# TensorE's expert loop rotated: down products first, slot addresses loaded two blocks ahead, covered waits dropped

## The reference, cut to what matters

```python
def moe(x2, w_router, router_bias, w1, w3, w2):
    expert_idx, gate_w = route(x2, w_router, router_bias)      # 2 of 16 experts for each of 512 tokens
    ...                                                        # tokens sorted by expert, padded to whole blocks
    def run_block(args):
        e, toks = args
        xb = x_pad[toks]
        h = jax.nn.silu(xb @ w1[e]) * (xb @ w3[e])             # 1024 -> 512, twice
        return h @ w2[e]                                       # 512 -> 1024
    yb = lax.map(run_block, (blk_e, slot_tok.reshape(n_blk, MOE_BLOCK)))
    y = yb.reshape(-1, D) * slot_gate[:, None]
    return jnp.zeros((N + 1, D), x2.dtype).at[slot_tok].add(y)[:N]
```

## Time and profile before

| what | value |
|---|---|
| median of 3 runs | 3668.87 us |
| lowest, highest | 3668.75, 3677.74 us |
| the profiled execution | 3650.51 us, of which its span 3648.8 us |
| first expert loop, first up product to last down product | about 687 to 1012 us |
| second expert loop | about 1718 to 2034 us |
| mean granted TensorE clock | 0.956 of full |

### The profile page before, as it was taken

How to read it: one execution, slowest core, us unless ns; L and a number is a source line. 1 busy time by engine, 2 the same in 40 slices (tenths; PEclk the granted TensorE clock), 3 DMA queues, 4 the chain that set the end, 5 groups by cost and what they waited for, 6 DMA issues and landing times. The chain is left out here.

```text
span 3648.8 us, 67482 instructions
## 1 busy us (share of the span) xinstructions
PE 3347.6 (92%) x25750; PEld 1870.7 (51%) x25751; DVE 1364.4 (37%) x2613; ACT 914.3 (25%) x1583; POOL 280.4 (8%) x207
## 2 busy tenths in 40 slices
PE   8998999789979989997899799999997788999998
PEld 5445444577754454445677444434444677444443
DVE  1564111456533751114566610101577455411102
ACT  1125111456521161113565400000114322100000
POOL 1000000322230000003222300000000000000000
PEclk9999999799989999998999899999999878999999
DMA  7111223599431103224997222253221000122221
GB/s 265 64 47 70 81 74 122 193 409 410 177 143 68 58 12 127 70 99 161 383 406 284 99 74 76 80 103 133 69 70 34 1 0 1 69 69 80 77 72 69
DMA packets 80474, 446.81 MB, mean 122 GB/s; under 512 B 19904, under 2 KB 20040, under 8 KB 33488
## 3 DMA queue, kind: packets, MB, share of 16 engines
q1 hardware_dynamic: 52128, 377.51, 27.4%
q0 software_dynamic: 25280, 64.54, 5.5%
q10 hardware_dynamic: 2928, 3.07, 0.2%
HBM read 412.05 MB, written 32.89 MB: 122 GB/s over the span
## 5 line engine op out<-in xcount | busy, mean ns | idle before, releaser
L909 PE MATMUL pb<-arena,streamed 128*128 128x512 f32 x1408 | 607.5, 594 | 4.1 <-DVE arena L1867 3.3
L909 PEld LDWEIGHTS pb<-arena,streamed 128*128 128x128 f32 x1408 | 268.0, 191 | 342.9 <-issue 334.9
L808 PE MATMUL pb<-arena,xT 128*32 x3008 | 359.1, 279 | 52.2 <-issue 30.7
L808 PE MATMUL pb<-streamed,xT 128*32 128x128 f32 x9024 | 361.5, 279 | 7.6 <-issue 7.6
L563 PE MATMUL pb<-xT,streamed 128*128 128x512 f32 x832 | 367.0, 599 | 0.0
L808 PEld LDWEIGHTS pb<-arena,xT 128*32 128x32 f32 x3008 | 326.8, 112 | 72.2 <-issue 66.2
L734 PE MATMUL pb<-xT,streamed 128*128 128x512 f32 x768 | 335.4, 595 | 2.5 <-ACT arena L1242 2.5
L808 PEld LDWEIGHTS pb<-streamed,xT 128*32 128x32 f32 x9024 | 330.8, 112 | 5.9 <-issue 5.8
L935 PE MATMUL pb<-arena,streamed 128*128 128x512 f32 x704 | 308.7, 601 | 9.0 <-DMA streamed<-in_w_tail 6.6
L1262 ACT ACTIVATE streamed<-arena 128x3072 f32 x94 | 260.2, 2768 | 57.3 <-SPq L386 39.7
L563 PEld LDWEIGHTS pb<-xT,streamed 128*128 128x128 f32 x832 | 158.9, 192 | 199.5 <-issue 199.4
(11 more groups left out here) (359 smaller groups left out, 3638.4 us busy)
## 6 DMA issues: line engine op xcount, KB each, us to landing
arena<-in_w_moe SPq DMA_DIRECT2D x192, 1024.0 KB, 11.8
streamed<-in_w_tail SPq DMA_DIRECT2D x87, 1024.0 KB, 4.8
streamed<-in_w_layer SPq DMA_DIRECT2D x78, 1024.0 KB, 4.8
xT<-xs_dram POOLq DMA_DIRECT2D x22, 512.0 KB, 8.6
ys_dram<-xT POOLq DMA_DIRECT2D x88, 128.0 KB, 9.1
xs_dram<-lnw POOLq DMA_DIRECT2D x12, 512.0 KB, 17.4
lnw<-in_ln_par POOLq DMA_DIRECT2D x4, 1024.0 KB, 5.9
rel_dram<-arena POOLq DMA_DIRECT2D x1, 4092.0 KB, 88.0
```

The lines of the kernel that those rows point to most:

```text
L808: last = mm(pb[m][r0:r0 + MOE_BLOCK, 0:FW], rows, w, start=(k == 0), stop=(k == KC - 1))
L909: last = mm(pb[3 * u + s][:], unit(w, u, k), xn[:, k * S:(k + 1) * S], start=(k == 0), stop=(k == KC - 1))
```

## The change

TensorE's loop is cut at another place of the same cycle. What stood in the loop as up(b), down(b-1), turn(b) stands there as down(b), turn(b+1), up(b+2); up 1 moves ahead of the loop and one up leaves the blocks behind it. The matmuls' order isn't changed by this. The branch of the loop now lies between an up and a down instead of between a turn and an up. The slot of block b+2 is loaded ahead of down(b), and kept in a list of registers; an iteration begins with three slot loads (two of blocks that the iteration before had, and one new). Three waits are dropped: `xsT_ready` but for the first block of a tile, `y_copied` in `down`, and `y_ready` in ScalarE's `copy_y` but for the last block. VectorE, GpSimd and SyncE have the same instructions as before.

```diff
--- before.py
+++ after.py
@@ -795,8 +795,9 @@
 
                 def up(b, s, off, tile):
 
-                    pe.wait_ge(xsT_ready, l * N_TILE + tile + 1)
-                    alone(pe)
+                    if s % COLS == 0:
+                        pe.wait_ge(xsT_ready, l * N_TILE + tile + 1)
+                        alone(pe)
                     for m, (relay, relayed) in enumerate(((w1_relay, w1_relayed), (w3_relay, w3_relayed))):
                         pe.wait_ge(relayed, l * N_BLK + b + 1)
                         alone(pe)
@@ -818,8 +819,6 @@
                 def down(b, s, off):
 
                     pe.wait_ge(hT_ready, l * N_BLK + b + 1)
-                    alone(pe)
-                    pe.wait_ge(y_copied, l * N_BLK + b + 1)
                     alone(pe)
                     pe.wait_ge(w2_relayed, l * N_BLK + b + 1)
                     alone(pe)
@@ -846,25 +845,26 @@
                     last = nc.tensor.transpose(pb[7][:, t * P:(t + 1) * P], last_sel[:, t * P:(t + 1) * P], identity)
                 last.then_inc(last_turned, 1)
                 turn(0)
+                up(1, 1, slot(1), 0)
+
+                def step(b, s, tile, now, ahead):
+
+                    if s == COLS - 2:
+                        transpose_xs(tile + 1)
+                    down(b, s, now)
+                    turn(b + 1)
+                    up(b + 2, s + 2, ahead, tile + (s + 2) // COLS)
+
                 with pe.Fori(0, N_TILE - 1) as i:
-                    off = slot(i * COLS)
-                    for s in range(1, COLS + 1):
-                        b = i * COLS + s
-                        ahead = slot(b)
-                        up(b, s, ahead, i + s // COLS)
-                        if s == COLS - 1:
-                            transpose_xs(i + 1)
-                        down(b - 1, s - 1, off)
-                        turn(b)
-                        off = ahead
-                off = slot(N_BLK - 3)
-                for s in (1, 2):
-                    b = N_BLK - 3 + s
-                    ahead = slot(b)
-                    up(b, s, ahead, N_TILE - 1)
-                    down(b - 1, s - 1, off)
-                    turn(b)
-                    off = ahead
+                    at = [slot(i * COLS + s) for s in range(2)]
+                    for s in range(COLS):
+                        at.append(slot(i * COLS + s + 2))
+                        step(i * COLS + s, s, i, at[s], at[s + 2])
+                at = [slot(N_BLK - 3 + s) for s in range(3)]
+                step(N_BLK - 3, 0, N_TILE - 1, at[0], at[2])
+                down(N_BLK - 2, 1, at[1])
+                turn(N_BLK - 1)
+                off = at[2]
                 down(N_BLK - 1, 2, off)
 
                 def last_tile(t):
@@ -1283,8 +1283,9 @@
 
                 def copy_y(b):
 
-                    act.wait_ge(y_ready, l * N_BLK + b + 2)
-                    alone(act)
+                    if b == N_BLK - 1:
+                        act.wait_ge(y_ready, l * N_BLK + b + 2)
+                        alone(act)
                     if b >= STORED:
                         n = (b - STORED) * MOE_BLOCK
                         for g in range(COLS):
```

## The result

The changed kernel takes 3735.31 us (median of 6 runs, 3726.13 to 3744.88), the kernel before beside it 3671.07 (6 runs, 3661.45 to 3677.74): a ratio of 1.0173 with an interval of 1.0158 to 1.0187, that is +64 us. The forecast was 3740 in a range of 3706 to 3766. The profiled execution of the changed kernel is of 3731.63 us, its span 3730.0. In the experiments one execution of the first (6761 us) and one of the second (7418 us) ran in a much slower state, and the ratios leave them out.

The account below looks back on a forecast made before the run. The loop was taken as bound by the array, and by TensorE's sequencer where its work exceeds what is queued; +64.9 us from gaps, +21 clock, -15 given back make +71, carried to the median: 3740 us, range 3706 to 3766.

Parts of the forecast that it names:

- Term 1: Slot loads of steps without row transposes, 44 in all: down products start 0.63 us later each, +27.7 us.
- Term 2: Slot loads ahead of the transposes of gathered rows, 22 in all: these start 0.36 us late each, +7.9 us.
- Terms 3 and 5: Loop returns, 20: down products 2.5 us late each, +50 us; loop entries and exits, 4: +1.3 each, +5.2 us.
- term 4: Transpose to up products: 1.49 us falls to 0.26 at 20 returns, -24.6 us; behind row transposes, 22 times, -1.3 us.
- Term 6: Dropped waits: TensorE's two are counted in other terms, ScalarE's y_ready goes at nothing; no new wait is made.
- Term 7, the clock: Half clock after idle at two in three of 24 places, +24 us, less two entry falls: +21 us.
- the rule as a rival (every return): The clock falls at every return: +12 us more, +15 if no weight wait is given back; 3752 to 3767, chance 0.13.
- Term 7, given back: Longer loops let weights arrive: three quarters of 14.1 us of waits go, -10.5 us, and three clock falls, -4.5 us.
- a longer lead of 1.0 us at the end of the up products: Sequencer 1.0 us ahead there too: 68 starts 0.4 us less late, -27 us, 3713 us; chance 0.05.
- "Hidden": Slot loads done while up products are still queued, so only gains stand: about -30 us, 3639 us; chance 0.05.
- "the clock holds at every return": No fall to half clock behind the loop's returns, so no +24 us: about 3716 us; chance 0.14.

Follow-up runs that it names:

- the first experiment: The kernel before with only the three dropped waits, its loop and slot loads unchanged: 3646.43 us, ratio 0.999.
- the second (7418 us): The changed kernel with the slot load back behind the transpose and two loads at the loop's head instead of three: 3661.14 us, ratio 1.0034.
- the run with four products more: The changed kernel with four unused matmuls ahead of each iteration's slot loads: 3707.03 us, ratio 1.0148; again 3727.92 us, ratio 1.0149.

## Why the prediction was right, and where its steps were off

- *The bound.* "By the sequencer wherever that is given more to do than it has work queued ahead" holds: with the load behind the transpose the ordinary blocks lose nothing, and with it behind the up products each loses 0.5 to 0.6 us in most cases, where the forecast had 0.63.
- *Term 1* (44 loads, +27.7): +26 measured. The start moved from 0.09 to between 0.60 and 0.68 us in most blocks.
- *Term 2* (22 places, 0.36 each, +7.9): +13.7. **This is the mis-sized term.** Without the long slot loads it is 9.6 - 4.6 = +5; with the y stores where they are, single loads took up to 1.5 and 2.0 us in the two traces. The trace of before had this only once, 885 ns at 717.4 us, and I took the duration from its median. The steps about the place were right, the assumption that an instruction keeps its price when it is moved was not.
- *Terms 3 and 5* (returns, entries, exits: 2.5 each): 24 places, 2.6 us in the mean, +60 with entries and exits. With term 4 that is +29, which is the forecast's sum for terms 3 to 5 (50 - 24.6 - 1.3 + 5.2).
- *Term 4* (-24.6 and -1.3): -31 with entries and exits, and 0.26 us is indeed the floor, in 81 of 92 places.
- *Term 6* (ScalarE's wait at nothing): the three dropped waits together gave -4 us of loop in the first experiment; ScalarE's alone has no run.
- *Term 7, the clock* (+21 - 4.5): +12 by the first traces and +21 by the second of each kernel (14.3 and 35.8 us); 12 of 24 places were followed by 1.2 GHz, not 16, and 11 of 24 in the second. The Trainium skill, "TensorE: Matmul & The Clock Gate", section "HAM oscillation", tells of idle that recurs in each tile and starts each next tile at the low clock; here it did so in half of the places, so the rule as a rival (every return) is ruled out. That idle is what brings the low clock here is shown by the run with four products more.
- *Term 7, given back* (-10.5 of the w3 waits): -6.8 in w3's, so half of them and not three quarters; -2.2 in w1's, contained in term 4's -31.
- *Not forecast:* stalls of 0.5 to 1.3 us in the block behind each loop, 10 us by the first traces. They are in the second trace of before as well (14 us), and absent in the run with later stores, so they aren't shown to be a cost of the change.

The sum of the terms was closer than its parts deserve: by the first traces 6 us too few for the row transposes, 5 too many for the clock, 4 too many taken off for the waits for weights, and no term for the stalls. It is luck, too, that 3740 lies within 5 us of the 3735.31: the loops, which the terms describe, grew by 83 and 80 us in the two pairs of traces, and the medians by 64. Moving the y stores takes 21 to 23 us of the 64 away, of which 9 are the row transposes' own; with them moved the time was 3712 us, at the lower end of the range.

The rivals: a longer lead of 1.0 us at the end of the up products is excluded by the down products' start at 892.94, 0.62 behind the last up product; with 1.0 in hand it would have been 0.2. The Trainium skill, "Advanced Engine Details and Errata", section "Engine Queue Depths", gives 64 instructions for TensorE, by an estimate from that page 0.87 us of up products. With that in hand the same start would have been about 0.35 behind, and in none of the 44 places, in either trace, is it under 0.60. "Hidden" is excluded by the 35 idles of each loop, "the clock holds at every return" by the 0.50 behind 763.33.

## What to carry to other kernels

A slot load, a branch and a standalone wait are work of TensorE's sequencer, and in this kernel they cost about what they take beyond the work that the array still has queued: read that lead at the very place (here 0.6 us at the end of the up products, 1.0 us at the transpose), and put them where it is long enough. A slot load cost nothing behind the transpose of an ordinary block, 0.24 us in the middle of the down products, 0.5 to 0.8 behind the up products, and its full length at a return; load once and carry the value in a register. Before an instruction that reads memory is moved, look at which transfers start at its new place, every time round the loop, since an iteration that repeats its timing can meet the same transfer again and again. And when a wait is removed from a loop that streams weights, count what of it the stream takes back: here 16 of some 37 us.

## What the runs showed of the hardware that I had not expected

- A TENSOR_LOAD of TensorE's sequencer takes 0.30 us, but in two traces of the changed kernel 16 took 0.77 to 2.03 us. All 16 stood in front of row transposes and began 1.94 us behind GpSimd's issue of a y store. The delay alone doesn't decide: 97 loads in the two traces began so, and the other 81 took 0.30 to 0.60, one of 0.30 (at 978.4 us) with 84 packets of GpSimd's queue under way. Nine more, begun 2.07 to 2.32 us behind an issue, took 0.60 to 0.95. Without the stores, or with them later, none in the loops took longer than 0.43. What the load and the store share isn't shown. In the kernel before, where loads begin 3.1 us and more behind such an issue, one load in 118 took longer than 0.6, and none in its second trace.
- A slot load in the middle of 32 down products isn't hidden: it lengthens them by about 0.1 us and the way from the transpose to the next up products by as much, 0.24 us in all by the sums.
- Idles of the same length (2.26 to 2.40 us) were followed by 1.2 GHz in some places and by 2.4 GHz in others. Where the up products ahead of the return had already waited for weights in the same block (759.07, 792.76 and 967.43 in the first trace), the fall came each time: at 763.33, 796.97 and 971.65, and at the same three places in the second trace and in that with later stores. What decides at the others stays open.
- Two executions of one kernel differ by 14 us in short stalls with the cause "issue" in the code just behind a loop.
